# First K and V group by token halves, its blocks split in the last expert, and four rows normalised by GpSimd

## The reference

```python
y = grouped_moe(u, router_w, router_bias, w_gu[0], w_down[0])
x = layer_norm(ALPHA * x + g2 * y, ln_g[0, 1], ln_b[0, 1])      # 512 x 1024
kv = x @ w_kv                                                    # 1024 x 1536
k_c, v_c = kv[:, 0:256], kv[:, 256:512]     # compressed over blocks of tokens
k_s, v_s, k_w, v_w = ...                    # the other two groups of 512 columns
```

## Time and profile before

| what | value |
|---|---|
| three runs, median | 1359.78 us (1354.26 to 1360.15) |
| profiled execution, its own time | 1353.95 us |
| its span, instructions | 1352.2 us, 17889 |
| mean granted TensorE clock | 0.967 |
| TensorE busy | 1241.9 us, 92% |
| VectorE, ScalarE, GpSimd busy | 1039.3, 774.5, 265.9 us |

### The profile page before, as it was taken

One profiled execution on the slowest core, in us unless ns is written; L12 is line 12 of the kernel. 1 busy time (PEld: TensorE's weight loads), 2 busy tenths in 40 slices (PEclk: granted clock), 3 DMA queues, 4 the chain that ended last, 5 costly groups with the idle time before them and its releaser, 6 DMA issues.

```text
span 1352.2 us, 17889 instructions
## 1 busy us (share of the span) xinstructions
PE 1241.9 (92%) x6523; PEld 959.8 (71%) x6524; DVE 1039.3 (77%) x1162; ACT 774.5 (57%) x1036; POOL 265.9 (20%) x317
## 2 busy tenths in 40 slices
PE   4999999599999999879998999999959999999985
PEld 4876677477777777658976777756747777777762
DVE  6787778789999898566856666643778999999857
ACT  3423224477777777573554555675247777777750
POOL 0112222200000000218005555445030000000020
PEclk9999999699999999889998999999979999999988
DMA  9877983599999999914852333134459999999961
GB/s 357 294 280 273 321 291 116 195 364 405 379 385 409 380 405 370 367 55 132 222 155 80 107 110 99 58 114 160 139 188 376 376 402 390 390 395 383 380 260 63
DMA packets 111950, 359.22 MB, mean 266 GB/s; under 512 B 8048, under 2 KB 16476, under 8 KB 111850
## 3 DMA queue, kind: packets, MB, share of 16 engines
q1 hardware_dynamic: 89992, 282.10, 57.0%
q0 software_dynamic: 17296, 60.38, 12.4%
q10 hardware_dynamic: 4594, 15.84, 2.9%
HBM read 329.94 MB, written 25.21 MB: 263 GB/s over the span
## 4 chain that ended last, share of the span: by engine, by line
PE 54%; DVE 16%; issue 11%; ACT 11%; DMA 5%; POOL 3%; ACTq 1%; SPq 0%; DVEq 0%; POOLq 0%
PE bank L237 13%; PE bank L238 13%; PE bank L239 13%; ACT w_hi L1392 4%; DMA ada<-in_ada_w_dram 3%; DVE acc L468 3%; PE bank L2267 2%; POOL prob L2489 2%; PE bank L2249 2%; DVE hh L1492 2%; PE bank L1431 2%; ACT xe_hi L1338 2%; PE bank L1321 1%; ACT prob L2390 1%; DVE w_lo L232 1%
## 5 line engine op out<-in xcount | busy, mean ns | idle before, releaser
L1398 DVE TENSOR_TENSOR w_lo<-raw,w_hi 128x2048 fp32r<-128x2048 f32 x189 | 435.7, 2309 | 56.9 <-ACT w_hi L1392 54.9
L1392 ACT ACTIVATE w_hi<-raw 128x2048 fp32r<-128x2048 f32 x189 | 362.5, 1919 | 77.6 <-PE bank L239 75.9
L237 PE MATMUL bank<-w_lo,xe_hi 128*128 128x512 f32 x512 | 211.8, 414 | 1.2 <-DVE xe_lo L1353 1.1
L239 PE MATMUL bank<-w_hi,xe_hi 128*128 128x512 f32 x512 | 203.6, 398 | 0.0
L238 PE MATMUL bank<-w_hi,xe_lo 128*128 128x512 f32 x512 | 203.6, 398 | 0.0
L227 ACT ACTIVATE w_hi<-raw 128x2048 fp32r<-128x2048 f32 x37 | 70.6, 1911 | 113.1 <-PE bank L239 86.8
L237 PE MATMUL bank<-u_lo,w_hi 128*128 128x512 f32 x288 | 119.2, 414 | 8.8 <-DVE q L2154 4.0
L1310 POOL DMA_INDIRECT xg<-scratch_u,tok x32 | 31.4, 982 | 480.1 <-PE bank L1321 455.0
L2489 POOL TENSOR_SCALAR prob<-prob,rsum,gates 128x512 f32<-128x512 f32 (+3 forms) x128 | 107.6, 854 | 92.5 <-DVE rsum L2457 92.4
L237 PEld LDWEIGHTS bank<-w_lo,xe_hi 128*128 128x128 f32 x512 | 97.2, 190 | 30.4 <-issue 8.5
L238 PE MATMUL bank<-u_hi,w_lo 128*128 128x512 f32 x288 | 115.6, 401 | 0.0
(11 more groups left out here) (331 smaller groups left out, 2252.0 us busy)
## 6 DMA issues: line engine op xcount, KB each, us to landing
raw<-in_w_gu_dram SPq DMA_DIRECT2D x128, 1024.0 KB, 7.9
raw<-in_w_down_dram SPq DMA_DIRECT2D x64, 1024.0 KB, 6.9
ada<-in_ada_w_dram POOLq DMA_DIRECT2D x48, 512.0 KB, 7.2
ada<-in_ada_w_dram SPq DMA_DIRECT2D x32, 512.0 KB, 3.8
scratch_y<-ye ACTq DMA_DIRECT2D x30, 512.0 KB, 7.3
raw<-in_conv_w_in_dram SPq DMA_DIRECT2D x12, 1024.0 KB, 14.2
mod_w<-in_ada_w_dram SPq DMA_DIRECT2D x8, 1024.0 KB, 14.0
raw<-in_w_kv_dram SPq DMA_DIRECT2D x6, 1024.0 KB, 8.8
```

Source lines behind the costliest of these rows:

```text
L237: nc.tensor.matmul(o, lh, rl, start=start, stop=False)
L239: return nc.tensor.matmul(o, lh, rh, start=False, stop=stop)
L1392: nc.scalar.activation(w_hi[:, hslot, :], raw[:, slot, :], ACT.Copy).then_inc(hi_done, 1)
L1398: nc.vector.tensor_tensor(w_lo[:, slot, :], raw[:, slot, :], w_hi[:, hslot, :].bitcast(F32), ALU.subtract).then_inc(lo_done, 1)
```

## The change

It has four parts, all at the end of layer 0.

1. Blocks 96 and 97 are split in the last expert: ScalarE's part before the copy of its output, VectorE's at the expert's end. SyncE issues their loads before the branch `over_sp`, the third load after it. Inside the branch, which overwrites the slots, both blocks are loaded and split again.
2. GpSimd normalises the rows (`norm_apply_pool`), not ScalarE.
3. ScalarE takes the root of row i + 1 between `u_t` and `u_hi` of row i. VectorE makes `u_lo` of row i - 2 ahead of the residual of row i, not after its statistics.
4. The first group goes by token halves: both blocks for rows 0 and 1, then both for rows 2 and 3, all in 256 columns. The transposes of row 3 come between the two blocks of the first half. The bias products wait for the residuals of two banks at a time. The `kv_mm` signals come in the last quarter.

```diff
@@ turn_act_cols
                 m.then_inc(x_full, 1)
+            if i + 1 < TT:
+                norm_root(act, moes[0].ln, i + 1)
             for h in range(2):
@@ 
+        def norm_apply_pool(pool, s, i):
+            pool.wait_ge(*s.coef.at(i + 1))
+            nc.gpsimd.tensor_scalar(xt[:, i, :], xt[:, i, :], ln_mv[:, i, 3:4], ln_mv[:, i, 4:5], ALU.mult, ALU.add
+                                    ).then_inc(s.norm.sem, 1)
@@ expert_act, expert_dve (last)
+                step_hi(act, s, pair, p, 4)
+                step_hi(act, s, pair, p, 5)
...
+            else:
+                step_lo(dve, s, pair, p, 4)
+                step_lo(dve, s, pair, p, 5)
@@ over_sp, over_act, over_dve, over_pe (inside the branch)
+                for b, src in again_blocks(s):
+                    sp.dma_start(shape_block(raw[:, b % NRAW, :], src), src).then_inc(o.weights_in, 16)
...
@@ moe_sp
+            for b, src in next_blocks[:2]:
+                load_block(sp, b, src)
             over_sp(sp, s)
-            for b, src in next_blocks:
+            for b, src in next_blocks[2:]:
                 load_block(sp, b, src)
@@ moe_pool
             if s.l == 0:
+                for i in range(TT):
+                    norm_apply_pool(pool, s.ln, i)
                 norm_rows_pool(pool, s.ln, turn_x)
@@ moe_act
-            step_hi(act, s, PAIRS - 1, 1, 4)
             for i in range(TT):
-                norm_root(act, s.ln, i)
+                if s.l == 1 or i == 0:
+                    norm_root(act, s.ln, i)
                 if s.l == 0:
-                    norm_apply(act, s.ln, i)
                     turn_act_cols(act, turn_x, mod_cols[:, 4, :], mod_cols[:, 5, :], i)
-            step_hi(act, s, PAIRS - 1, 1, 5)
             step_hi(act, s, PAIRS - 1, 1, 6)
@@ moe_dve
-            step_lo(dve, s, PAIRS - 1, 1, 4)
...
                     norm_coef(dve, s.ln, i - 1)
+                if i >= 2 and s.l == 0:
+                    turn_dve_cols(dve, turn_x, i - 2)
                 end_residual(dve, s, i)
                 norm_stats(dve, s.ln, i)
...
-                elif i >= 2:
-                    turn_dve_cols(dve, turn_x, i - 2)
...
-            step_lo(dve, s, PAIRS - 1, 1, 5)
@@ moe_pe
-            if s.l == 0:
-                turn_pe_cols(pe, turn_x, TT - 1)
@@
+        def kv_first_pe(pe):
+            for half in range(2):
+                pe.wait_ge(*turn_x.lo.at(TT * (half + 1)))
+                t = slice(half * 2 * P, (half + 1) * 2 * P)
+                for kh in range(2):
+                    b = B_KVG[0] + kh
+                    pe.wait_ge(lo_done, b + 1)
...
+                    for m in range(4):
+                        c_ = slice(m * P, (m + 1) * P)
+                        if half + kh == 0 and m % 2 == 0:
+                            pe.wait_ge(*moes[0].res.at(2 * TT - 2 + m))
+                            for o in bank[m:m + 2]:
+                                nc.tensor.matmul(o[:], identb[:], before_b[:, 0:1].to_broadcast([P, SEQ]), start=True,
+                                                 stop=False, skip_group_check=True)
...
+                        if half == 1 and kh == 1 and m < 3:
+                            mm.then_inc(kv_mm, 1)
+                    if half == 1:
+                        mm.then_inc(blk_used, 1)
+                    elif kh == 0:
+                        turn_pe_cols(pe, turn_x, TT - 1)
```

More of the change, by code:

```diff
@@ L1551, in hybrid_trunk, with again_blocks @@
         OVER_STEPS = 6 + 2 * TT
+        def again_blocks(s):
+            return [(B_KV + b, kv[b]) for b in range(2)] if s.l == 0 else []
         def if_over(eng, s):
@@ L1565, in over_sp @@
                 sp.wait_ge(blk_used, s.b0 + EBLK * NE)
+                for b, _ in again_blocks(s):
+                    sp.wait_ge(lo_done, b + 1)
                 over_load(sp, s, o, 0)
@@ L1599, in over_pe @@
                 pe.wait_ge(o.added, TT * NE + 1)
+                pe.wait_ge(o.h, TT * NE + len(again_blocks(s)))
         def over_act(act, s):
@@ L1611, in over_act @@
                 act.wait_ge(o.step, OVER_STEPS)
+                act.wait_ge(o.weights_in, 32 * NE + 16 * len(again_blocks(s)))
+                for b, _ in again_blocks(s):
+                    nc.scalar.activation(w_hi[:, b % NSPLIT, :], raw[:, b % NRAW, :], ACT.Copy).then_inc(o.ht, 1)
         def over_dve(dve, s):
@@ L1648, in over_dve @@
                                               in1=xt[:, i, :], op0=ALU.mult, op1=ALU.add))
+                for j, (b, _) in enumerate(again_blocks(s)):
+                    dve.wait_ge(o.ht, TT * NE + j + 1)
+                    V.tensor_tensor(w_lo[:, b % NRAW, :], raw[:, b % NRAW, :], w_hi[:, b % NSPLIT, :].bitcast(F32),
+                                    ALU.subtract).then_inc(o.h, 1)
         def moe_sp(sp, s, next_blocks):
@@ L1870, in hybrid_trunk @@
         x_saved = sem("x_saved")
[L1872 to L1897, removed]
@@ new lines, in kv_first_pe @@
+        def kv_first_pe(pe):
[5 more added lines that the diff above has]
+                    pe.wait_ge(lo_done, b + 1)
+                    wh = w_hi[:, b % NSPLIT, :].rearrange("p (k n) -> p k n", k=4)
+                    wl = w_lo[:, b % NRAW, :].rearrange("p (k n) -> p k n", k=4)
+                    for m in range(4):
[5 more added lines that the diff above has]
+                                                 stop=False, skip_group_check=True)
+                        for kk in range(4):
+                            k = 4 * kh + kk
+                            nc.tensor.matmul(bank[m][:, t], wh[:, kk, c_], u_lo[:, k, t], start=False, stop=False,
+                                             skip_group_check=True)
+                            nc.tensor.matmul(bank[m][:, t], wl[:, kk, c_], u_hi[:, k, t], start=False, stop=False,
+                                             skip_group_check=True)
+                            mm = nc.tensor.matmul(bank[m][:, t], wh[:, kk, c_], u_hi[:, k, t], start=False,
+                                                  stop=(k == KD - 1), skip_group_check=True)
+                        if half == 1 and kh == 1 and m < 3:
[4 more added lines that the diff above has]
+                        turn_pe_cols(pe, turn_x, TT - 1)
@@ L1903, in kv_pe @@
                 pe.wait_ge(kv_v, 4)
+            if g == 0:
+                kv_first_pe(pe)
+                return
             for kh in range(2):
@@ L1908, in kv_pe @@
                 wl = w_lo[:, b % NRAW, :].rearrange("p (k n) -> p k n", k=4)
-                if g == 0:
-                    kv_first_pe(pe, kh, wh, wl)
-                    continue
                 for m in range(4 if g == 0 else 2):
```

## The result

The changed kernel takes 1350.44 us (median of 7 runs, 1346.43 to 1353.68), the kernel before 1357.89 us over the same runs (7, 1354.26 to 1360.15). The ratio is 0.9950, with a 95% interval of 0.9938 to 0.9962: 0.5% or 6.8 us faster, forecast 6.2 (the two medians themselves lie 7.45 us apart). The profiled execution took 1352.85 us, which is more than its median; that of before took 1353.95, less than all seven timed ones. The two profiles side by side therefore show less than the medians do, and stretches are compared here, not spans.

A forecast was written before the change was run, and what follows sets the result against it. TensorE, 92% busy, was taken as the bound, waiting for row 3. A gain of 6.5 us less 0.3 given back made -6.2: 1353.6 us from the earlier median of 1359.78 (1347.8 on the execution read), range 1347.4 to 1360.

The forecast's parts named there:

- The bound: End of layer 0: TensorE, 92% busy, loses 5.5 us waiting for row 3 and 0.9 us to slow transposes.
- Nothing gained or lost until turn(2): Row loop: TensorE's order (combine, then turn) is the limit, so turn(2) comes at 591.75 against 591.80 us before.
- added up to 1.24 us to one engine or the other: Row loop: GpSimd's row meets VectorE's two-operand u_lo, one goes first, and the other is up to 1.24 us late.
- The slower rival: Rows 0 to 2 each wait for the exclusion, at 3.8 us a row: 1.3 us slower, 1361.1 us; chance 0.06.
- The reordered group: First K and V group by token halves: from 593.0 it ends at 617.55, before 624.05 us; gain 6.5 us.
- The place that I called the tightest: ScalarE's root ahead of u_hi holds u_hi(1) until about 589.9, and u_lo(1), which TensorE's first half needs at 592.9.
- the 0.6 us that I had there: Row loop: VectorE's u_lo(0) ends at 585.6, which starts the residual of row 2 0.6 us late.
- The splits cost nothing: Last expert: early splits of blocks 96 and 97 fit idle time of ScalarE and VectorE, hidden by TensorE's 24 down products.
- What is given back later: Behind the first group: flat subtractions and a later load lose 0 to 0.6 us each; 0.3 us taken for both.
- three deadlines: Flat subtractions, k_hi behind GpSimd's last row, and the block landing: each under 2 us left, none over 0.6 us late.
- the first rival: New waits take the gain back: three deadlines each slip 1 us, leaving -3.5 us, 1356.3 us; chance 0.20.
- Two of the signs that I had named for being wrong: Signs named: GpSimd rows over 2 us, turn(2) behind 593, or a wait over 2 us between 620 and 660.

The follow-up runs named there:

- Run b: Changed kernel with the first group back in its old order (row 3 transposed first, block by block); ratio 0.9997 to the kernel before.
- Run i: Changed kernel with u_lo of row i - 2 back behind the statistics of row i; ratio 0.9971 to the kernel before.
- run h: Kernel before with only blocks 96 and 97 split in the last expert, all else as before; ratio 0.9989 to the kernel before.
- d: Changed kernel with SyncE issuing the third group's two loads ahead of the four row saves; ratios 0.9930 and, again, 0.9942 to the kernel before.
- e: Changed kernel with the last compression block's load issued ahead of the eight K copies; ratio 0.9935 to the kernel before.
- a: Changed kernel measured again without any edit; ratio 0.9957 to the kernel before.
- c: Changed kernel with the rows normalised by ScalarE again, not GpSimd; ratio 0.9942 to the kernel before.

## Why the prediction was right, and where it was not

- **The bound.** Right: TensorE's wait for row 3 and the low clock behind it were the whole gain. Run b takes the reorder away and has none (0.9997).
- **Nothing gained or lost until turn(2).** Nearly: turn(2) keeps its place in TensorE's queue, 0.35 us later. GpSimd's row cost 1.20 us as estimated, but the exclusion by u_lo came in each of three rows with 1.02 us, where I had added up to 1.24 to one engine or the other. For row 2 I let GpSimd go first; it went second, and that is the 0.3 us. The slower rival (each row waits d, turn(2) comes 3d late) had the exclusion right, but not its size (2.22 us a row for 3.8) nor its sum: d was 1.02 us in rows 1 and 2, and turn(2) came 0.35 us late, not 2 to 3 us, since TensorE's own combines cover most of it (it waited 0.64 us for row 2, before 0.34). Run i, where row 2 takes 1.20 us again, has the 0.3 us back.
- **The reordered group.** Forecast from turn(2) to block 98: 591.75 to 617.55, 25.8 us. Measured 25.10. The bias products and the first half block took 6.28 us for 6.55, row 3's transposes 0.79 for 1.05. The place that I called the tightest was not: u_lo of row 1 ended at 589.86, 2 us before turn(2) did. It went ahead of GpSimd and not behind it, and row 2's residual (583.63) waited for TensorE, not for u_lo of row 0 (ended at 582.98), so the 0.6 us that I had there did not come. What makes this place safe is the early u_lo: with u_lo behind the statistics (run i) TensorE waits 3.36 us there. The 5.65 us for a half block is not quite half of the 11.39 us that I took it from (5.70); measured were 16.88 us for three, 5.63 each.
- **The splits cost nothing.** Right in the total (run h: 0.9989), and the copy of the output still waits for TensorE's last down product (it starts at 565.19, 1.04 us of waiting for L239). Not foreseen: they hold up GpSimd's gathers.
- **What is given back later.** The step that failed: "Loss: 0 to 0.6 us more ... All else behind group 0 follows TensorE." I walked three deadlines (flat subtractions, k_hi, the third group's first load), and all three held. GpSimd's eight operations even ended at 629.0, not between 632.4 and 633.4. (The third group's second load landed just as ScalarE came for it at 641.62, after 0.96 us of idle time; in the kernels of runs d and e ScalarE has the same 0.96 us there by waiting for TensorE, so it cost nothing.) The one that broke is the fourth, the last compression block, which stands behind the K copies on SyncE's queue. The walk does not name it, and it does not follow TensorE: it was issued 2.45 us later against block 98 and took 12.7 us to landing, before 10.0. The loss was 3.45 us (2.9 and 3.7 in runs a and c), of which 1.6 us are lower clock behind the waits, a term that the sum did not have. In the seam that leaves 3.15 us of gain, closer to the first rival's sum (3.5 us kept) than to the forecast, by one late transfer and not by three slips. Two of the signs that I had named for being wrong did show: rows on GpSimd over 2 us, and a wait over 2 us between 620 and 660 (ScalarE's, 3.31 us).
- **The total.** -6.2 us forecast, -6.8 measured (-5.2 to -8.4 by the interval), though the seam of the two profiles differs by 3.15 us only. Against the kernels of runs b and h, whose low clock lasted longer and whose totals are those of the kernel before, the changed seam (147.00 and 146.80) is 4.7 to 5.5 us shorter. The other 1.3 us or more I can't place: the stretches before and behind the seam scatter by several us from execution to execution. So the closeness of the total is in part luck: the forecast had a loss that was 3 us too small and a gain in the group that was 0.7 us too small, and what made up the rest no stretch shows. The forecast on the median, 1353.6 us, was 3.2 us above the 1350.44 measured; 1.9 us of that lie in the three runs before, whose median was higher than that of the seven.

## What to carry to other kernels

When an engine's work is pulled ahead of a late input, list every transfer whose start hangs on some other engine (here SyncE's loads behind GpSimd's last row), since these don't move along: compare each landing, not each issue, with the new deadline, and put loads that need nothing ahead of stores that wait. Before moving work to GpSimd, look at which two-operand VectorE work starts by the same semaphore; here the move was worth nothing, and the reorder everything. Where totals scatter by several us, lengths between two fixed instructions settle changes of half a microsecond, if the length itself repeats: the third column did to 0.03 us, the first did not.

## What the runs showed of the hardware

VectorE's splits, which read two operands from SBUF, hold up GpSimd's gathers too. In the changed kernel VectorE splits blocks 96 and 97, and GpSimd issues the gathers of the experts' rows:

```profile
560.51 2.29 DVE L1405 TENSOR_TENSOR w_lo<-raw,w_hi 128x2048 fp32r<-128x2048 f32 x1 [3.92 <-ACT w_hi L1399]
...
564.18 2.29 DVE L1405 TENSOR_TENSOR w_lo<-raw,w_hi 128x2048 fp32r<-128x2048 f32 x1 [1.38 <-ACT w_hi L1399]
...
561.17 2.44 POOL L1718 DMA_INDIRECT yg<-scratch_y,yrow  x1 [0.31 <-issue]
...
563.92 0.93 POOL L1718 DMA_INDIRECT yg<-scratch_y,yrow  x1 [0.30 <-issue]
...
565.16 2.13 POOL L1718 DMA_INDIRECT yg<-scratch_y,yrow  x1 [0.30 <-issue]
```

A gather that took 0.93 to 0.94 us without a split beside it takes 2.44 and 2.13 us when it starts during one. It ends 0.8 us behind the split (563.61 and 567.29, for splits that end at 562.80 and 566.47), a little less than a gather's own time. All twelve profiles with the early splits show it, with gathers of 1.89 to 3.05 us. It is not mutual: the gather of 563.92 was under way when the split of 564.18 started, and both kept their own lengths, 0.93 and 2.29 us. So the wait seen for GpSimd's tensor operations holds for its indirect DMA instructions as well, but only for one that starts while the split runs.

A branch not taken cost TensorE 0.2 to 1.6 us, differently in each execution of the same code (0.50 and 1.06 us in two of the changed kernel), and no wait of another engine explains it.
